# Value products one turn later in a fused attention layer, transposed probabilities in two slots, forget weights loaded first

## What is computed

```python
h = rms_norm(x, norm_pre_g[layer])
proj = jnp.einsum('bsd,de->bse', h, w_in[layer])
q_a, k_a, v_a, g_a, f_a, q_b, k_b, v_b, g_b = jnp.split(proj, offsets, axis=-1)
log_f = jax.nn.log_sigmoid((f_a + fox_forget_b[layer]).astype(jnp.float32))
y_a = fox_attention(...q_a, k_a, v_a, log_f...)     # logits + F[t] - F[s], causal softmax
y_a = merge_heads(y_a) * jax.nn.silu(g_a)
y_b = moba_attention(...q_b, k_b, v_b, slopes)      # logits - slope * distance, causal softmax
y_b = merge_heads(y_b) * jax.nn.silu(g_b)
y = jnp.einsum('bse,ed->bsd', jnp.concatenate([y_a, y_b], axis=-1), w_out[layer])
x = x + rms_norm(y, norm_post_g[layer])
```

## Time and profile before

| | us |
|---|---|
| median of 3 runs | 150.39 (149.98 to 150.87) |
| the profiled execution | 150.02 |
| its span | 148.2 |
| TensorE busy | 138.7 (94%) |
| VectorE busy | 108.3 (73%) |
| ScalarE busy | 94.1 (64%) |
| GpSimd busy | 52.6 (36%) |

### The profile page before, as it was taken

How to read it: one execution, slowest core, us unless ns; L and a number is a source line. 1 busy time by engine, 2 the same in 40 slices (tenths; PEclk the granted TensorE clock), 3 DMA queues, 4 the chain that set the end, 5 groups by cost and what they waited for, 6 DMA issues and landing times.

```text
span 148.2 us, 2971 instructions
## 1 busy us (share of the span) xinstructions
PE 138.7 (94%) x1060; PEld 129.4 (87%) x1060; DVE 108.3 (73%) x234; ACT 94.1 (64%) x193; POOL 52.6 (36%) x74
## 2 busy tenths in 40 slices
PE   7679999999999999999999999999999999999930
PEld 7558999999999999999999999999999888898830
DVE  0359837899999999879898888687879774222591
ACT  5279588668967578797576686676838373234340
POOL 2069200000000061039194857557290936020411
PEclk9999999999999999999999999999999999999998
DMA  4899999399865999953544444434290000000034
GB/s 85 252 338 336 350 404 342 85 352 268 286 191 202 383 398 332 316 209 87 197 146 142 142 142 148 139 109 143 66 383 15 2 0 0 0 4 0 0 142 142
DMA packets 9725, 26.96 MB, mean 182 GB/s; under 512 B 1384, under 2 KB 2416, under 8 KB 9456
## 3 DMA queue, kind: packets, MB, share of 16 engines
q1 hardware_dynamic: 9120, 25.57, 50.6%
q10 hardware_dynamic: 592, 1.22, 2.2%
HBM read 25.73 MB, written 1.06 MB: 181 GB/s over the span
## 4 chain that ended last, share of the span: by engine, by line
PE 86%; DMA 5%; issue 3%; POOL 2%; DVE 1%; ACT 1%; POOLq 1%; DVEq 0%; ACTq 0%
PE bank L830 46%; PE bank L840 14%; PE bank L987 11%; PE bank L941 6%; PE bank L924 5%; DMA wf<-in_w_f 4%; DMA gpre_col<-in_g_pre 2%; PE bank L932 1%; PE bank L933 1%; PE bank L931 1%; POOL x_t L361 1%; POOL h L358 1%; POOLq L72 1%; ACT squares L539 0%; PE bank L887 0%
## 5 line engine op out<-in xcount | busy, mean ns | idle before, releaser
L563 DVE TENSOR_TENSOR w_lo<-raw,w_hi 128x1024 fp32r<-128x1024 f32 (+1 forms) x33 | 43.9, 1335 | 4.6 <-ACT w_hi L375 4.3
L375 ACT ACTIVATE w_hi<-raw 128x1024 fp32r<-128x1024 f32 (+1 forms) x33 | 34.5, 1057 | 6.3 <-PE bank L830 2.6
L830 PE MATMUL bank<-h_hi,w_hi 128*128 128x256 f32 x128 | 36.4, 285 | 0.0
L830 PE MATMUL bank<-h_lo,w_hi 128*128 128x256 f32 x128 | 35.7, 279 | 0.0
L830 PE MATMUL bank<-h_hi,w_lo 128*128 128x256 f32 x128 | 35.7, 279 | 0.0
L309 POOL TENSOR_TENSOR bias<-squares,causal 128x256 f32<-128x256 f32 (+1 forms) x8 | 12.9, 1627 | 37.5 <-DMA squares<-decay_rows_scratch 37.5
L830 PEld LDWEIGHTS bank<-h_hi,w_hi 128*128 128x128 f32 x128 | 24.1, 188 | 1.2
L830 PEld LDWEIGHTS bank<-h_lo,w_hi 128*128 128x128 f32 x128 | 24.0, 188 | 0.2
L326 POOL TENSOR_TENSOR probs<-probs,row_inv 128x256 f32<-128x256 f32 (+1 forms) x16 | 12.9, 827 | 31.7 <-DVE row_inv L705 31.7
L830 PEld LDWEIGHTS bank<-h_hi,w_lo 128*128 128x128 f32 x128 | 24.1, 188 | 0.0
L830 PE MATMUL bank<-xg_hi,w_hi 128*128 128x256 f32 x64 | 17.8, 278 | 0.0
(11 more groups left out here) (121 smaller groups left out, 304.9 us busy)
## 6 DMA issues: line engine op xcount, KB each, us to landing
raw<-in_w_units SPq DMA_DIRECT2D x30, 512.0 KB, 4.8
raw_out<-in_w_out SPq DMA_DIRECT2D x4, 512.0 KB, 6.0
raw<-in_w_out SPq DMA_DIRECT2D x4, 512.0 KB, 3.5
h<-in_x SPq DMA_DIRECT2D x2, 512.0 KB, 7.9
squares<-decay_rows_scratch ACTq DMA_DIRECT2D x1, 1024.0 KB, 6.0
x_t<-in_x SPq DMA_DIRECT2D x1, 1024.0 KB, 6.5
raw<-in_w_units SPq DMA_DIRECT2D x3, 256.0 KB, 5.3
out<-x_t SPq DMA_DIRECT2D x3, 256.0 KB, 2.0
```

Source lines behind the costliest of these rows:

```text
L375: nc.scalar.activation(w[0][:, s, 0:width], raw[:, s, 0:width], ACT.Copy).then_inc(s_hi, 1)
L563: nc.vector.tensor_tensor(w[1][:, s, 0:width], raw[:, s, 0:width], w[0][:, s, 0:width].bitcast(F32), ALU.subtract).then_inc(s_lo, 1)
L830: last = nc.tensor.matmul(dst, stationary(a, j), moving(b, j), start=n == 1, stop=n == count * len(PASSES))
```

## The change

Three things are changed.

1. The load of `wf` is issued on ScalarE's queue right behind the first activation (a Sqrt that loads the table), ahead of the wait for the norm gains and of the rounding of x.
2. The value products of a pair come one turn later, and stand between scores and key unit: turn i becomes Q(i), T(i-2), S(i-1), V(i-3), K(i), and turn 2 has no value products. V(5) comes right behind turn 7. The gating moves with them, in front of the key's low part on VectorE (`gated(i - 3)` ahead of `key_low(i)`); `y_high` in a turn is that of pair i-4 and `y_low` that of pair i-3. The loop over pairs 2 and 3 on GpSimd is written out.
3. The transposed probabilities get two slots, used in turn, since V(i-3) now reads one set after T(i-2) has been written out.

```diff
-        p_t0 = [sb(f"p_t0_{n}", [P, 2, SEQ], F32R) for n in PARTS]
-        p_t1 = [sb(f"p_t1_{n}", [P, 2, P], F32R) for n in PARTS]
+        p_t0 = [sb(f"p_t0_{n}", [P, 2, 2, SEQ], F32R) for n in PARTS]
+        p_t1 = [sb(f"p_t1_{n}", [P, 2, 2, P], F32R) for n in PARTS]
...
-            with pool.Fori(2, FOX_PAIRS) as i:
+            for i in range(2, FOX_PAIRS):
                 norm_probs(i - 1)
                 pool.wait_ge(s_logits, 4 * i)
                 fox_bias(i)
-                y_low(i - 2)
+            y_low(FOX_PAIRS - 4)
             with pool.Fori(FOX_PAIRS, PAIRS) as i:
                 norm_probs(i - 1)
                 pool.wait_ge(s_logits, 4 * i)
                 moba_bias(i)
-                y_low(i - 2)
+                y_low(i - 3)
+            y_low(PAIRS - 3)
             norm_probs(PAIRS - 1)
...
             nc.scalar.activation(root[:, 0:1], ones[:, 0:1], ACT.Sqrt).then_inc(s_table, 1)
+            act.dma_start(wf[:, :, :], w_f).then_inc(s_wf_in, 16)
             act.wait_ge(s_g_in, 16)
...
-                if c == 0:
-                    act.dma_start(wf[:, :, :], w_f).then_inc(s_wf_in, 16)
...
                 if first == 0 and not fresh:
-                    y_high(i - 3)
+                    y_high(i - 4)
...
             unit_high(2, 16 * (UNITS // RING + 1), UNITS - 1)
+            y_high(PAIRS - 4)
+            probs_high(PAIRS - 2, 0)
+            unit_high(3, 16 * (UNITS // RING + 1), UNITS)
             y_high(PAIRS - 3)
-            probs_high(PAIRS - 2)
-            unit_high(3, 16 * (UNITS // RING + 1), UNITS)
             exps(PAIRS - 1)
...
                 if first != 1:
                     row_inverses(i - 1)
+                if not isinstance(i, int):
+                    dve.wait_ge(s_ylo, i - 3)
+                if not isinstance(i, int) or i == 3:
+                    gated(i - 3)
                 key_low(i)
...
-                if first == 0:
-                    if not (isinstance(i, int) and i == 2):
-                        dve.wait_ge(s_ylo, i - 2)
-                    gated(i - 2)
...
+            dve.wait_ge(s_ylo, PAIRS - 3)
+            gated(PAIRS - 3)
             unit_low(2, UNITS + 3)
...
                 scores(i - 1, 1 - b)
+                if i > 3:
+                    pe.wait_ge(s_y, 2 * i - 6)
+                if not first:
+                    values(i - 3)
                 key(i, b)
-                if not first:
-                    pe.wait_ge(s_y, 2 * i - 4)
-                values(i - 2)
...
+            pe.wait_ge(s_y, 2 * PAIRS - 6)
+            values(PAIRS - 3)
             pe.wait_ge(s_olo, OUT_OWN)
```

More of the change, by code:

```diff
@@ L459, in _, with probs_high @@
             unit_high(1, 80, V_UNITS + 6)
-            def probs_high(i):
+            def probs_high(i, b):
                 act.wait_ge(s_pt, i + 1)
-                nc.scalar.activation(p_t0[0][:, :, :], pt0_ps, ACT.Copy).then_inc(s_pthi, 1)
-                nc.scalar.activation(p_t1[0][:, :, :], pt1_ps, ACT.Copy).then_inc(s_pthi, 1)
+                nc.scalar.activation(p_t0[0][:, b, :, :], pt0_ps, ACT.Copy).then_inc(s_pthi, 1)
+                nc.scalar.activation(p_t1[0][:, b, :, :], pt1_ps, ACT.Copy).then_inc(s_pthi, 1)
             def exps(i):
@@ L504, in attend @@
                 if first == 0:
-                    probs_high(i - 2)
+                    probs_high(i - 2, b)
                 if first != 2:
@@ L520, in _ @@
             attend(2, 0, 16 * (QK_0 // RING + 2), fresh=True)
-            attend(3, 1, 16 * (QK_0 // RING + 3))
+            attend(3, 1, 16 * (QK_0 // RING + 3), fresh=True)
             with act.Fori(2, PAIRS // 2) as it:
@@ L526, in _ @@
             unit_high(2, 16 * (UNITS // RING + 1), UNITS - 1)
+            y_high(PAIRS - 4)
+            probs_high(PAIRS - 2, 0)
+            unit_high(3, 16 * (UNITS // RING + 1), UNITS)
             y_high(PAIRS - 3)
-            probs_high(PAIRS - 2)
-            unit_high(3, 16 * (UNITS // RING + 1), UNITS)
             exps(PAIRS - 1)
             y_high(PAIRS - 2)
-            probs_high(PAIRS - 1)
+            probs_high(PAIRS - 1, 1)
             y_high(PAIRS - 1)
@@ L685, in scores_there, with probs_low @@
                 dve.wait_ge(s_bias, 2 * i + 2)
-            def probs_low(i, scored=None):
+            def probs_low(i, b, scored=None):
                 for n, (dst, src) in enumerate(((p_t0, pt0_ps), (p_t1, pt1_ps))):
@@ L691, in probs_low @@
                         scores_there(scored)
-                    nc.vector.tensor_tensor(dst[1][:, :, :], src, dst[0][:, :, :].bitcast(F32),
+                    nc.vector.tensor_tensor(dst[1][:, b, :, :], src, dst[0][:, b, :, :].bitcast(F32),
                                             ALU.subtract).then_inc(s_ptlo, 1)
@@ L732, in attend @@
                 if first == 0:
-                    probs_low(i - 2, i - 1)
+                    probs_low(i - 2, b, i - 1)
                 if first != 1:
@@ L758, in _ @@
                     attend(2 * it + b, b)
+            dve.wait_ge(s_ylo, PAIRS - 3)
+            gated(PAIRS - 3)
             unit_low(2, UNITS + 3)
-            probs_low(PAIRS - 2, PAIRS - 1)
+            probs_low(PAIRS - 2, 0, PAIRS - 1)
             row_logits(PAIRS - 1, 0)
@@ L766, in _ @@
             gated(PAIRS - 2)
-            probs_low(PAIRS - 1)
+            probs_low(PAIRS - 1, 1)
             dve.wait_ge(s_ylo, PAIRS - 1)
@@ L940, in values @@
                     dst = pv_ps if t == 0 else pv_ps[:, :, P:SEQ]
-                    last = nc.tensor.matmul(dst, v[:, x * TT + t, i * P:(i + 1) * P], (p_t0, p_t1)[t][z][:, :, :],
+                    last = nc.tensor.matmul(dst, v[:, x * TT + t, i * P:(i + 1) * P], (p_t0, p_t1)[t][z][:, i % 2, :, :],
                                             start=n == 0, stop=n == len(order) - 1)
```

## The result

The changed kernel takes 152.08 us in the median (151.55 to 152.97, 4 runs), the kernel before 150.19 us beside it (149.79 to 150.87, 4 runs): 1.0158 times the time, with a 95% interval from 1.0108 to 1.0207. The forecast was 152.8 us in 151.2 to 153.9, slower. The profiled execution took 152.57 us against 150.02 before: +2.55 us, where the sum of the prediction said +2.4.

What follows compares the result with a forecast made beforehand. TensorE, busy 94% of 148.2 us, was taken as the bound. Gain 0.52 swallowed to 0, plus 1.05 + 0.53 + 0.72 = 2.30, plus 0.1 for restarts: +2.4, giving 152.4 profiled, 152.8 us median, range 151.2 to 153.9.

Steps and rivals of the forecast that it cites:

- Part 2: Turn 3: with V(0) gone from turn 2, TensorE idles at T(1) until GpSimd's norm of pair 1; cost 1.05 us.
- the wait swallows the start: At T(1): the wait for the norm absorbs the whole 0.52 us gained by loading the forget weights first.
- that in turn hangs on ScalarE's table load at 61.93, not on TensorE: Before T(1): pair 0's norm follows the table load before the first exponentials, so T(1) stays at 76.0 us.
- The prediction's own sign of being wrong: The prediction would be wrong if T(1) starts near 75 us, or TensorE shows no idle time behind 110 us.
- Part 3: Tail: V(5) waits for VectorE's gating of pair 4, wanted at 115.29 and done at 115.82; cost 0.53 us.
- Part 4: Tail: output product of pairs 4 and 5 waits for y's low part of pair 5; cost 0.72 us.
- Part 1: Start: loading forget weights first removes TensorE's idle before unit 0's last piece; 0.52 us, bounds 0 and 0.52.
- (a): Only the first wait, at T(1), counts, as the tail's chains run earlier: 151.4 to 152.0 us; chance 0.15.
- (b): Not slower, as pair 1's norm comes earlier with TensorE: 149.9 us (chance 0.05) or 150.2 to 151.1 (0.08).
- (d): Start: the forget weights land no earlier, which changes nothing in the sum; chance about 0.25.
- (c): VectorE's next w_lo stretches the norm, so T(1) comes up to 0.98 us later: 153.8 us; chance 0.10.

Runs made afterwards that it cites:

- the second profile: The changed kernel itself, nothing further edited, measured again with six more runs against the kernel before: 151.49 us, ratio 1.0118.

## Why the prediction was right, and where not

**Part 2, V(0) leaves turn 2: right in place and cause, somewhat large.** Forecast 1.05, measured 0.75 at T(1) and 0.18 in the turns behind. The prediction took T(1)'s slack as nil, from 75.89 against 76.00. That was true of that execution, in which a weight load was 0.89 us late. In the two profiles of the kernel with only the load moved T(1) has 0.44 us to spare (norm from 72.62, 1.61 long; T(1) at 74.67). 1.05 - 0.44 = 0.61, and with 0.14 from the norm's end to the transposes it is the 0.75 measured. The 0.18 has another cause, the query units, which the prediction had at the same length in both orders. The slack was read from a single execution, on a chain in which a DMA comes late in some of them.

**Part 2, "the wait swallows the start": wrong.** The step that failed is "that in turn hangs on ScalarE's table load at 61.93, not on TensorE". In the profile at hand the reading was right, but by 0.2 us only: the table load ends at 61.93 + 1.28 = 63.21, and the first exponentials also need VectorE's row maxima, which follow TensorE's scores. Of these the last that is needed ended at 63.02 in the kernel before:

```profile
62.94 0.08 DVE L699 DVE_READ_ACCUMULATOR2_ANT neg_max<- 128x1 f32 x1
```

In the changed kernel's profile the load was in time and the table load over at 62.85, so the same row maxima released the exponentials at 63.06. The query's rounding ahead of the table load waited for TensorE there too. And where the weight load comes late, its issue still moves with TensorE (44.0 to 45.3 us behind unit 1). So the whole chain moves with TensorE, apart from the time that one load takes. The prediction's own sign of being wrong, T(1) near 75 us, came in the second profile (74.58), beside a wait of 0.70 us as in the first (0.71).

**Part 3: right.** Forecast V(5) wanted at 115.29 and released at 115.82; it starts at 115.78 in the trace, behind the gating, which starts at 114.85 and not at 114.94. Forecast 0.53, measured 0.60 by stages, and 0.59 when undone.

```profile
114.85 0.88 DVE L722 TENSOR_TENSOR y<-bank,gate 64x256 f32<-64x256 f32 x2
```

**Part 4: right, a fifth short.** Forecast: low part ready 3.84 us behind T(6); measured 123.46 - 119.68 = 3.78. The output product is 0.81 late (3.93 against 3.12), and the stage is 0.93 longer; 0.90 comes back when undone. The 0.1 between them is about what the sum allowed for all restarts together.

**Part 1: the term that was mis-sized.** Bounds 0 and 0.52, taken from TensorE's last idle stretch. The late weights held ScalarE's whole queue for 1.07 us, and the piece of x and the roundings of unit 1 stood behind. Between the kernel before and the second profile of the changed one, unit 1's start moves by 1.13 us: 0.62 from the third piece of unit 0 to the last (7.91 to 9.40 against 7.69 to 8.56), 0.29 from there to unit 1 (9.40 to 10.42 against 8.56 to 9.29), and 0.22 because the third piece starts earlier. So 0.9 us is what the late forget weights held up, with 0.52 forecast. Over the profiles unit 1 starts 0.6 to 1.6 us earlier, with the one exception of the last section. The prediction looked at the products of unit 0 and not at what is queued behind the rounding that waited.

The load also left 2.04 us sooner, where the forecast had "at least 0.6 to 0.8". In the program its issue stands behind the Sqrt activation, but ScalarE's queue sent it off at 1.25 us, before that activation had started:

```profile
1.25 0.39 ACTq L386 DMA_DIRECT2D wf<-in_w_f  x1
...
2.48 0.20 ACT L385 ACTIVATE root<-ones 128x1 f32<-128x1 f32 x1
```

**Why the sum agreed all the same.** In the profiled execution the start gained nothing, since TensorE ran its first products at half pace (last section). So +2.55 met +2.4. In other executions the start does gain: +2.45 - 1.13 is +1.3, near what the second measurement found (151.49 against 150.07). The agreement of the profiled pair was partly luck: a gain counted as nothing for a wrong reason was nothing for another, and the 0.3 us by which Part 2 was too large met 0.18 in the turns, which was not in the sum, and 0.28 in Parts 3 and 4, for which it had 0.1.

**Rival (a), (b), (d):** the tail's waits are real, so (a) falls. (b) is right that the norm comes with TensorE, but all of it shifts alike, so it doesn't save the wait. (d) falls: the weights had landed by 4.96 us, when GpSimd's copy starts, where it was 8.64.

**Rival (c) falls, and the order of starts fits.** The norm takes 1.61 us, as ever, and the weight rounding that starts over its end takes longer, 1.73 us where it takes 1.22 alone:

```profile
72.39 1.22 DVE L564 TENSOR_TENSOR w_lo<-raw,w_hi 128x1024 fp32r<-128x1024 f32 x1
...
75.07 1.73 DVE L564 TENSOR_TENSOR w_lo<-raw,w_hi 128x1024 fp32r<-128x1024 f32 x1 [0.53 <-ACT w_hi L376]
```

The bias of pair 1, which starts at 66.85 while a rounding runs (from 66.44), takes 3.96 us for two operations, where that of pair 2 takes 2.97. The Trainium skill ("SBUF — State Buffer", "SBUF: two separate sides") says that of two such operations the one that starts first keeps the shared ports to its end and the other is blocked. By that rule the norm, whose two instructions start at 74.11 and an estimated 0.8 us later, could not be stretched by a rounding at 75.07; the trace agrees. It doesn't separate what the rounding owes to the norm from what it owes to the next bias, which starts at 75.68. The prediction had called (c) likely by this rule without asking which comes first.

## To carry to other kernels

When work is moved out of a turn, look for the next cross-engine wait that it had been covering, and take that wait's slack from more than one execution where a DMA stands in its chain. When an instruction that waits heads an in-order queue, price what is queued behind it, not only the consumer's idle time. And where single executions scatter by 1%, compare stages of the traces: here fourteen profiles of twelve kernels tell apart tenths of a microsecond which the medians hardly could.

## Hardware behaviour that was not expected

**The first products can run at half pace in one execution and not in the next.** In the first profile of the changed kernel:

```profile
5.31 0.76 PE L843 MATMUL bank<-w_hi,xg_hi 128*128 128x256 f32 x2 [0.54 <-ACT w_hi L407]
5.88 0.63 PE L843 MATMUL bank<-w_hi,xg_lo 128*128 128x256 f32 x2
6.30 0.63 PE L843 MATMUL bank<-w_lo,xg_hi 128*128 128x256 f32 x2
...
9.33 0.64 PE L843 MATMUL bank<-w_hi,xg_hi 128*128 128x264 f32 x2
```

A pair starts every 0.43 us: 256 columns in 0.214 us, which is 1.2 GHz. The same place in the second profile of the same kernel:

```profile
5.25 0.77 PE L843 MATMUL bank<-w_hi,xg_hi 128*128 128x256 f32 x2 [0.48 <-ACT w_hi L407]
5.82 0.50 PE L843 MATMUL bank<-w_hi,xg_lo 128*128 128x256 f32 x2
6.15 0.40 PE L843 MATMUL bank<-w_lo,xg_hi 128*128 128x256 f32 x2
6.39 0.40 PE L843 MATMUL bank<-w_hi,xg_hi 128*128 128x256 f32 x2
```

From the third pair on one starts every 0.24 us, the pace that such pairs keep later on, at the 2.4 GHz level. Ahead of both stand the same sixteen products on constants (from 0.99 us, 3.78 us long) and then half a microsecond of idle time; the granted clock reads 1.00 in both from 0 to 20 us. So this column does not show it; only the spacing of the products does. The slow stretch had ended by 6.6 us in all the other profiles and lasted to about 10.2 in this one. Unit 1 started 1.29 us later than in the second profile (10.58 against 9.29). Of this an estimated 0.2 us is the weights of the third piece, rounded from 7.41 us against 7.22, and 1.1 us the pace. The whole gain of the early load was gone with it. The Trainium skill ("TensorE: Matmul & The Clock Gate", "What's actually happening") says that the number of products at the lower clock at a kernel's start varies between runs of the same kernel; the two profiles agree. What decides it here was not tried.

**A small load can take as long as a large one.** The 32 KB of forget weights took 2.8 to 3.7 us from issue to landing in the twelve profiles in which they were issued at 1.25 us, and 5.3 and 4.6 us when issued at 3.29 and 3.89, with loads of x and of weight units under way; a weight unit of 512 KB takes 4.8 us in the median. Between the two kernels of the prediction the issue moved by 2.04 us and the landing by 3.6. That the other loads are the reason is likely and was not tested.
